# The skip term of a state-space mixer: from an identity matmul on TensorE to an add on GpSimd

## What is computed

```python
def ssd_chunked(xdt, a, bm, cm):
    ...
    y_diag = jnp.einsum("bgrcls,bcsgrp->bclgrp", M, X)
    ...
    y_off = jnp.einsum("bclgn,cbgrpn,bgrcl->bclgrp", Cc, prev, jnp.exp(A_cs))
    return (y_diag + y_off).reshape(b, s, h, p)

def ssd_mixer(...):
    ...
    y = y_fwd + y_bwd + ssd_D.astype(jnp.float32)[:, None] * xf
    y = y.reshape(b, s, D_INNER).astype(xBC.dtype)
    return rms_norm(y * jax.nn.silu(z), ssd_norm_w)
```

## Time and profile before

| | us |
|---|---|
| median of 3 runs | 924.48 (923.9 to 928.98) |
| profiled execution, its own time | 932.96 |
| its span | 931.2 |
| PE busy | 909.1 (98% of the span) |
| DVE busy | 668.8 (72%) |
| ACT busy | 512.1 (55%) |
| POOL busy | 79.1 (8%) |
| granted TensorE clock, mean | 0.995 |

### The profile page before, as it was taken

The page is one execution under the profiler, slowest core; times in us unless marked ns, Lnnn a source line. Parts: engine busy times, 40 slices in busy tenths (PEclk is TensorE's granted clock), DMA queues, the critical chain, the costliest instruction groups (busy, mean ns, idle before and its releaser), DMA issues.

```text
span 931.2 us, 18104 instructions
## 1 busy us (share of the span) xinstructions
PE 909.1 (98%) x7450; PEld 866.4 (93%) x7450; DVE 668.8 (72%) x918; ACT 512.1 (55%) x696; POOL 79.1 (8%) x56
## 2 busy tenths in 40 slices
PE   5999999899999999999999999999998999999998
PEld 3899998789888899999999999989898999999998
DVE  6878998997699988778766554546875866666642
ACT  2566656677877874345655434455675654444430
POOL 0133000000465330000000000000000000000000
PEclk9999999999999999999999999999998999999999
DMA  9764554766312245666755555543422345555650
GB/s 377 304 235 160 202 182 137 271 219 234 136 65 79 88 139 221 258 240 208 258 190 180 183 186 192 194 174 136 137 92 91 126 147 182 185 186 190 218 197 18
DMA packets 25085, 168.00 MB, mean 180 GB/s; under 512 B 2869, under 2 KB 4533, under 8 KB 5049
## 3 DMA queue, kind: packets, MB, share of 16 engines
q1 hardware_dynamic: 23760, 164.90, 50.0%
q10 hardware_dynamic: 1256, 2.12, 0.6%
HBM read 165.95 MB, written 1.06 MB: 179 GB/s over the span
## 4 chain that ended last, share of the span: by engine, by line
PE 86%; DVE 5%; ACT 4%; DMA 3%; issue 1%; SPq 0%; DVEq 0%; ACTq 0%
PE bank L1861 85%; DMA raw<-w_stream 2%; DMA adas<-w_stream 1%; DVE cvt L1338 1%; ACT whi L573 1%; DVE wlo L1104 1%; DVE acc L1149 1%; PE bank L2129 1%; DVE p L1316 0%; ACT prob L724 0%; PE bank L2153 0%; DVE hlo L1207 0%; ACT kw__113 L822 0%; DVE wlo L1114 0%; ACT rqx L981 0%
## 5 line engine op out<-in xcount | busy, mean ns | idle before, releaser
L1861 PE MATMUL bank<-hhi,whi 128*128 128x256 f32 (+1 forms) x1364 | 384.5, 284 | 1.1 <-DVE hlo L1207 0.6
L1861 PE MATMUL bank<-hlo,whi 128*128 128x256 f32 (+1 forms) x1352 | 377.1, 279 | 0.0
L1861 PE MATMUL bank<-hhi,wlo 128*128 128x256 f32 (+1 forms) x1352 | 375.4, 279 | 0.0
L1104 DVE TENSOR_TENSOR wlo<-raw,whi 128x2048 fp32r<-128x2048 f32 (+1 forms) x130 | 299.1, 2302 | 100.3 <-ACT whi L573 98.3
L573 ACT ACTIVATE whi<-raw 128x2048 fp32r<-128x2048 f32 (+1 forms) x132 | 250.6, 1899 | 100.5 <-PE bank L1861 73.5
L1861 PEld LDWEIGHTS bank<-hhi,whi 128*128 128x128 f32 (+1 forms) x1364 | 255.0, 188 | 12.1 <-issue 11.0
L1861 PEld LDWEIGHTS bank<-hlo,whi 128*128 128x128 f32 (+1 forms) x1352 | 255.1, 189 | 0.1
L1861 PEld LDWEIGHTS bank<-hhi,wlo 128*128 128x128 f32 (+1 forms) x1352 | 254.4, 189 | 0.0
L1861 PE MATMUL bank<-fhi,whi 128*128 128x256 f32 x432 | 121.4, 281 | 0.0
L1861 PE MATMUL bank<-flo,whi 128*128 128x256 f32 x432 | 121.4, 281 | 0.0
L1861 PE MATMUL bank<-fhi,wlo 128*128 128x256 f32 x432 | 121.4, 281 | 0.0
(11 more groups left out here) (296 smaller groups left out, 1327.6 us busy)
## 6 DMA issues: line engine op xcount, KB each, us to landing
raw<-w_stream SPq DMA_DIRECT2D x147, 1024.0 KB, 4.9
adas<-w_stream SPq DMA_DIRECT2D x8, 1024.0 KB, 8.7
xres<-x_t SPq DMA_DIRECT2D x1, 1024.0 KB, 10.1
out<-oute SPq DMA_DIRECT2D x8, 128.0 KB, 3.8
tabs<-tabs_in_dram ACTq DMA_DIRECT2D x1, 641.0 KB, 8.7
tabs<-tabs_in_dram ACTq DMA_DIRECT2D x1, 512.0 KB, 3.6
hankel<-bucket_rows ACTq DMA_DIRECT2D x1, 512.0 KB, 5.8
cols<-cols_in_dram ACTq DMA_DIRECT2D x1, 325.0 KB, 8.1
```

Source lines behind the costliest of these rows:

```text
L1104: nc.vector.tensor_tensor(out=wlo[:, c % RING, 0:n], in0=raw[:, r % RING, 0:n], in1=whi[:, c % RING, 0:n].bitcast(f32), op=ALU.subtract)\
L1861: return nc.tensor.matmul(out, lhsT, rhs, start=start, stop=stop)
```

## The change

GpSimd gets a new step, `skip_added(i)`: it waits until DVE's first pass over `yt` (yor_done) is finished and adds the scaled x to `yt`. It stands in POOL's loop ahead of `decayed`. DVE's second pass (the sum with `side[5]`) now waits for this step instead of for DVE's own first pass. On PE the identity matmul is gone, and so is its wait for skip_done; the first of the eight heads' matmuls now opens the bank. Since skip_done now counts both kinds of steps, a small function gives the count.

```diff
+        def skips(i):
+
+            return (3, 5)[i] if i < 2 else 5 + i
...
+            def skip_added(i):
+
+                g, t = i % NG, i // NG
+                pool.wait_ge(yor_done, i + 1)
+                pool.wait_ge(skip_done, skips(i) - 1)
+                y = yt[:, i % 2, :].rearrange("p (j l) -> p j l", j=4)
+                nc.gpsimd.tensor_tensor(out=y, in0=y, in1=xcv[:, 4 * g:4 * g + 4, t * P:(t + 1) * P],
+                                        op=ALU.add).then_inc(skip_done, 1)
...
+                if i >= 2:
+                    skip_added(i - 2)
                 decayed(i)
                 if i < NG:
                     skipped(i)
...
             for i in (6, 7):
+                skip_added(i)
                 weighted(i)
                 squares(i)
...
                 nc.vector.tensor_tensor(out=y, in0=side[3][:, :], in1=y, op=ALU.mult).then_inc(yor_done, 1)
-                dve.wait_ge(yor_done, i + 1)
+                dve.wait_ge(skip_done, skips(i))
                 dve.wait_ge(yd_done, i + 1)
                 nc.vector.tensor_tensor(out=y, in0=side[5][:, :], in1=y, op=ALU.add).then_inc(ydr_done, 1)
...
                 pe.wait_ge(w_done, i + 1)
-                pe.wait_ge(skip_done, g + 1)
-                mm(side[5][:, :], tab("ident"), xcv[:, 4 * g:4 * g + 4, t * P:(t + 1) * P], True, False)
                 for h in range(HG):
                     o = side[5][(h % 2) * HD:(h % 2 + 1) * HD, (h // 2) * P:(h // 2 + 1) * P]
                     f = (g * HG + h) * HD
-                    last = mm(o, xtok[:, t, f:f + HD], kw_[:, h, :], False, h >= HG - 2)
+                    last = mm(o, xtok[:, t, f:f + HD], kw_[:, h, :])
                 last.then_inc(yd_done, 1)
```

## The result

The changed kernel took 943.4 us (median of 4 runs, 940.0 to 946.9) beside 924.2 for the kernel before: a ratio of 1.0202, 95% interval 1.0146 to 1.0259. It is slower, as forecast, but by 19 us where 10 were forecast, and 943.4 lies above the range. A second series of the same kernel, run later beside the experiments, gave 1.0191 (1.0141 to 1.0242).

The account below looks back on a forecast made before the run. DVE and PE were both taken as full, with PE waiting for DVE: 10.1 + 1.4 + 2.3 - 1.55 - 0.85 = 11.4 us, less 0.95 gives 10.4; on the 924.48 median, 935 us, range 927 to 941.

Parts of the forecast that it names:

- moving work off one of them: PE's eight identity matmuls removed: seven priced at nothing, the last, behind w_done of iteration 7, to give 0.95 us.
- the wait that was put into the other's program: DVE's second pass waiting for POOL's add: 1.44 us stall per iteration, seven before w_done of iteration 7, 10.1 us.
- the margin between the last producer and its consumer: DVE's masks to PE's states, rounds 5 to 8: DVE ahead by only 0.15 to 0.70 us, so PE waits beyond that.
- blocks whichever VectorE passes from SBUF now stand there: Collisions with POOL: xd on gate passes 1.4 us, `skipped` on rounds 3 and 4 2.3, credit for sslo 0.85.
- the granted clock fell after single waits of PE: Rival for PE's idling in each round: clock falls to the lower level, 14 us or more extra, 949 or more; chance 0.06.

Follow-up runs that it names:

- e5: The changed kernel with DVE's first pass over yt moved ahead of later_decays, so DVE works while POOL adds; stage 109.7 us, ratio 1.0153.
- e13: The changed kernel once more, unaltered, on the chip of the following runs; stage 123.4 us, ratio 1.0191.

## What to carry over

Where two engines are full in a stage, as here, moving work off one of them gained nothing, and the wait that was put into the other's program cost its full length; the margin between the last producer and its consumer tells which case it is. When a GpSimd pass is put into a chain with VectorE, price not the pass but its train: everything behind it on GpSimd moves too, and blocks whichever VectorE passes from SBUF now stand there, here many short ones worse than the long ones that it used to meet (+10.4 and -4.7 us). If such a step must be, give VectorE bank-reading work between the signal and the wait (e5 took back 13.9 of 16.9 us up to `so`, 11.8 up to rcol). And follow a gain in a stage up to the next meeting of the engines: an engine that is early may only wait there.

## What was unexpected of the hardware

The products of the long loops ran at one of two steps, which changes from execution to execution and within one, with a granted clock of 1.00 in both. The loop of `gu` in the kernel before, and in the kernel after (PE timeline, one product each 0.118 and 0.113 us):

```profile
800.04 0.28 PE L1861 MATMUL bank<-hhi,wlo 128*128 128x256 f32 x1
800.16 0.28 PE L1861 MATMUL bank<-hhi,whi 128*128 128x256 f32 x1
800.28 0.28 PE L1861 MATMUL bank<-hlo,whi 128*128 128x256 f32 x1
```
```profile
812.00 0.28 PE L1877 MATMUL bank<-hhi,whi 128*128 128x256 f32 x1
812.11 0.28 PE L1877 MATMUL bank<-hlo,whi 128*128 128x256 f32 x1
812.22 0.28 PE L1877 MATMUL bank<-hhi,wlo 128*128 128x256 f32 x1
```

The lengths come in two groups each over all eighteen traces: `m1` about 82.5 or 85.5 us (first to last `fr` of ACT), `m2` 86.7 or 90.1 and `dn` 59.5 or 61.8 (first to last product with fhi and whi), `gu` 110.2 or 114.4 (first to last `fr` of DVE); together up to 13 us, more than most effects studied here. e13, the same code as after, had the short `m1` and `m2`, and after the long ones. In each trace `m1` and `m2` went together, and so did `gu` and `dn`. What chooses the step stays open. The lower clock of the earlier trace rows is a second thing of this kind: from the end of `m2` to the first `fr` of `gu` the execution of before took 149.3 us, and the other seventeen 144.0 to 144.9.

Besides, the granted clock fell after single waits of PE of 2.5 to 4.8 us (0.59 in 280 to 285 us), although PE had full work before and behind them, but not after each such wait (e13); and a GpSimd pass of two fp32 operands of 128x512 takes 1.29 to 1.30 us undisturbed, in all eight instances.
